# Even attention with turns two and values three items behind the scores, band values in another place, and the last update shared with TensorE

## The reference

```python
def trunk(x, pos, caches, w):
    for l in range(DEPTH):                                   # DEPTH = 2
        g = w['norm_g'][l]
        ff_a = swiglu(rms_norm(x, g[0]), ...)
        x = x + 0.5 * rms_norm(ff_a, g[1])
        h = rms_norm(x, g[2])
        mix, st = even_mixer(h, ...) if l % 2 == 0 else odd_mixer(h, ...)
        x = x + rms_norm(mix, g[3])
        ff_b = swiglu(rms_norm(x, g[4]), ...)
        x = x + 0.5 * rms_norm(ff_b, g[5])
    return x, new_cache_rows
```

```python
s = einsum('bqhd,bkhd->bhqk', q, k) * HEAD_SCALE + bias
p = softmax(where(mask, s, -1e30))
out = einsum('bhqk,bkhd->bqhd', p, v)
```

## Time and profile before

| | |
|---|---|
| time, median of 3 runs | 1887.73 us (1887.36 to 1887.78) |
| the profiled execution, time | 1887.22 us |
| its span, first to last instruction | 1885.4 us |
| TensorE (PE) busy | 1868.0 us, 99% |
| VectorE (DVE) busy | 1529.7 us, 81% |
| ScalarE (ACT) busy | 1183.4 us, 63% |
| GpSimd (POOL) busy | 303.0 us, 16% |

### The profile page before, as it was taken

The page is one execution under the profiler, slowest core; times in us unless marked ns, Lnnn a source line. Parts: engine busy times, 40 slices in busy tenths (PEclk is TensorE's granted clock), DMA queues, the critical chain, the costliest instruction groups (busy, mean ns, idle before and its releaser), DMA issues.

```text
span 1885.4 us, 38908 instructions
## 1 busy us (share of the span) xinstructions
PE 1868.0 (99%) x15552; PEld 1819.0 (96%) x15552; DVE 1529.7 (81%) x2102; ACT 1183.4 (63%) x2281; POOL 303.0 (16%) x317
## 2 busy tenths in 40 slices
PE   9999999999999999999999999999999999999997
PEld 9999999999669999999999999999997999999997
DVE  7889998688773878999868799997757487999975
ACT  7566666765685656666676666666738555656564
POOL 0002020300452100202020002020335200020202
PEclk9999999999999999999999999999999999999999
DMA  4233322422311222322241323233241222232322
GB/s 163 90 107 96 107 96 91 128 69 102 126 46 46 63 95 90 101 102 96 101 129 46 101 97 105 90 112 104 99 126 44 72 65 102 84 118 86 113 93 73
DMA packets 59043, 177.95 MB, mean 94 GB/s; under 512 B 7072, under 2 KB 11504, under 8 KB 58736
## 3 DMA queue, kind: packets, MB, share of 16 engines
q1 hardware_dynamic: 55504, 166.50, 26.3%
q0 software_dynamic: 2128, 7.80, 1.3%
q10 hardware_dynamic: 1232, 1.16, 0.2%
HBM read 168.26 MB, written 5.36 MB: 92 GB/s over the span
## 4 chain that ended last, share of the span: by engine, by line
PE 97%; DMA 1%; DVE 1%; ACT 1%; issue 0%; ACTq 0%; POOL 0%; POOLq 0%; DVEq 0%
PE psum L930 30%; PE psum L928 30%; PE psum L929 30%; PE psum L1295 1%; PE psum L1281 1%; PE psum L1414 1%; PE psum L1199 1%; DMA out_kpe<-kpe_all 1%; PE psum L1397 1%; PE psum L1256 1%; PE psum L1369 1%; PE psum L1245 0%; DMA x<-in_x 0%; PE psum L982 0%; PE psum L1175 0%
## 5 line engine op out<-in xcount | busy, mean ns | idle before, releaser
L928 PE MATMUL psum<-xhi,w_hi 128*128 128x272 f32 x1552 | 451.1, 291 | 1.8 <-DVE xlo L2335 1.7
L930 PE MATMUL psum<-xhi,w_lo 128*128 128x272 f32 x1552 | 447.8, 289 | 0.0
L929 PE MATMUL psum<-xlo,w_hi 128*128 128x272 f32 x1552 | 446.4, 288 | 0.0
L928 PEld LDWEIGHTS psum<-xhi,w_hi 128*128 128x128 f32 x1552 | 292.3, 188 | 5.2 <-issue 2.3
L929 PEld LDWEIGHTS psum<-xlo,w_hi 128*128 128x128 f32 x1552 | 292.2, 188 | 0.5
L930 PEld LDWEIGHTS psum<-xhi,w_lo 128*128 128x128 f32 x1552 | 291.7, 188 | 0.0
L781 DVE TENSOR_TENSOR w_lo<-w_raw,w_hi 128x1024 fp32r<-128x1024 f32 (+1 forms) x208 | 236.7, 1138 | 64.3 <-ACT w_hi L778 61.7
L929 PE MATMUL psum<-corner,w_hi 128*128 128x272 f32 x864 | 249.9, 289 | 0.0
L930 PE MATMUL psum<-corner,w_lo 128*128 128x272 f32 x864 | 249.8, 289 | 0.0
L928 PE MATMUL psum<-corner,w_hi 128*128 128x272 f32 x864 | 248.7, 288 | 0.0
L778 ACT ACTIVATE w_hi<-w_raw 128x1024 fp32r<-128x1024 f32 (+1 forms) x208 | 206.2, 991 | 39.9 <-PE psum L930 38.5
(11 more groups left out here) (366 smaller groups left out, 4918.9 us busy)
## 6 DMA issues: line engine op xcount, KB each, us to landing
w_raw<-in_w_gate_up SPq DMA_DIRECT2D x172, 512.0 KB, 4.1
w_raw<-in_w_down SPq DMA_DIRECT2D x96, 384.0 KB, 3.7
w_raw<-in_w_down SPq DMA_DIRECT2D x32, 256.0 KB, 2.7
w_raw<-in_even_in SPq DMA_DIRECT2D x16, 512.0 KB, 4.2
w_raw<-in_odd_in SPq DMA_DIRECT2D x10, 512.0 KB, 4.3
w_raw<-in_even_out SPq DMA_DIRECT2D x8, 512.0 KB, 4.3
w_raw<-in_odd_out SPq DMA_DIRECT2D x8, 512.0 KB, 4.2
out_band_kv<-qkvb POOLq DMA_DIRECT2D x1, 2176.0 KB, 9.9
```

What stands on the lines that cost most here:

```text
L928: nc.tensor.matmul(out, s_hi, m_hi, start=first, stop=False, skip_group_check=skip)
L929: nc.tensor.matmul(out, s_hi, m_lo, start=False, stop=False, skip_group_check=skip)
L930: return nc.tensor.matmul(out, s_lo, m_hi, start=False, stop=last, skip_group_check=skip)
```

## The change

Three things are changed together.

1. In even attention, TensorE's round becomes `even_scores(n)`, `turn(n - 2)`, `values(n - 3)`, and begins at n = 2 with the turn of item 0 ahead of the scores of item 3. ScalarE's round becomes `copy_turned(n - 2)`, `exponentials(n)`; the outputs follow one round sooner on ScalarE and VectorE. The rounds are one fewer, so the fourth early part of the output projection stands behind the loop. VectorE's order of maxima and inverses and GpSimd's order stay as they are.
2. `vB` moves to the place of `w_sum` and `rstd`, which are not in use in attention. ScalarE's copies into it no longer wait for the two stores, but for the last scaling of the mixer's tiles (`mix_scaled`).
3. In the last update, four tiles (`TAIL`) of the second half are added by TensorE: it multiplies x by the identity into PSUM, then y * r by the identity on top, tile by tile. ScalarE copies each sum to x and stores the tiles in two pairs from its own queue. VectorE multiplies all eight tiles as before and adds the other four.

```diff
--- before.py
+++ after.py
@@ -256,6 +256,7 @@
 JOBS_IN = (1, 5, 7, 9)
 
 
+TAIL = 4
 A0 = {"even": 0, "odd": N_EVEN}
 O0 = {"even": 0, "odd": len(EVEN)}
 
@@ -315,7 +316,8 @@
         w_raw = place("w_raw", [P, 4, D], F32)
         w_hi = place("w_hi", [P, 4, D], F32R)
         w_lo = place("w_lo", [P, 4, D], F32R)
-        gate_even = place("gate_even", [P, 4, TH], F32, at=cursor[0])
+        w_sum_at = cursor[0]
+        gate_even = place("gate_even", [P, 4, TH], F32, at=w_sum_at)
         w_sum = place("w_sum", [P, 3, D // 2], F32)
         rstd_at = cursor[0]
         rstd = place("rstd", [P, T], F32)
@@ -365,7 +367,7 @@
         probsE = [place("probsE%d" % i, [P, 2, w], F32, at=pr_at + o) for i, (w, o) in
                   enumerate(((384, 7168), (512, 10240), (384, 0)))]
         probsTE = [place("probsTE%d" % i, [P, 2, 512], F32, at=pr_at + o) for i, o in enumerate((3072, 14336))]
-        vB = place("vB", [P, 4, NH * HD], F32, at=arena + 17408)
+        vB = place("vB", [P, 4, NH * HD], F32, at=w_sum_at)
         vB_new = place("vB_new", [P, NH * HD], F32, at=pr_at + 18432)
         bias = [place("bias%d" % p, [P, 2, 2 * P], F32, at=kn_at + 3200 * p) for p in range(4)]
         vB_cache = place("vB_cache", [P, 2, NH * HD], F32, at=qr_at)
@@ -491,6 +493,9 @@
         k_ready = sem("k_ready")
         k_copied = sem("k_copied")
         v_ready = sem("v_ready")
+        tail_scaled = sem("tail_scaled")
+        tail_summed = sem("tail_summed")
+        tail_out = sem("tail_out")
         v_copied = sem("v_copied")
         band_in = sem("band_in")
         vb_turned = sem("vb_turned")
@@ -913,9 +918,9 @@
 
             c = len(SUBS)
             for H in range(2):
-                for k, count in ((0, 2), (2, 2), (4, 2), (6, 2)) if H == 0 else ((0, 2), (2, 2), (4, 2), (6, 1), (7, 1)):
+                for k, count in ((0, 2), (2, 2), (4, 2), (6, 2)) if H == 0 else ((TAIL, 2), (6, 1), (7, 1)):
                     some = slice(k, k + count)
-                    sp.wait_ge(x_ready, 16 * (c - 1) + 8 * H + k + count)
+                    sp.wait_ge(x_ready, 16 * (c - 1) + 8 * H + k - TAIL * H + count)
                     sp.dma_start(outs["y"][:, some, HALF[H]], x[:, some, HALF[H]]).then_inc(y_stored, 16)
             sp.wait_ge(y_stored, 16 * (KD + 1))
 
@@ -1319,18 +1324,19 @@
                                 first = False
                     mm.then_inc(pv_done, 1)
 
-                for n in range(3, N_EVEN + 4):
-                    if n < N_EVEN:
+                for n in range(2, N_EVEN + 3):
+                    if 2 < n < N_EVEN:
                         even_scores(n)
-                    if 3 <= n < N_EVEN + 3:
-                        turn(n - 3)
-                    if n >= 4:
-                        values(n - 4)
+                    if n < N_EVEN + 2:
+                        turn(n - 2)
+                    if n >= 3:
+                        values(n - 3)
                     if n in (N_EVEN, N_EVEN + 2):
 
                         pe.wait_ge(exp_done, N_EVEN if n > N_EVEN else N_EVEN - 1)
                     if n >= N_EVEN:
                         out_early(s, n - N_EVEN)
+                out_early(s, 3)
 
             def swa_scores(s, n):
 
@@ -1609,6 +1615,13 @@
                 out_projection(s)
             post_sum(len(SUBS) - 1, 1)
             post_last(len(SUBS) - 1, 1)
+            pe.wait_ge(y_scaled, 2 * KD * ffn_no(len(SUBS)))
+            for m in range(TAIL):
+                nc.tensor.matmul(psum[:, m, 0:TH], ident[:], x[:, m, HALF[1]], start=True, stop=False)
+            for m in range(TAIL):
+                pe.wait_ge(tail_scaled, m // 2 + 1)
+                nc.tensor.matmul(psum[:, m, 0:TH], ident[:], y[:, m, HALF[1]], start=False,
+                                 stop=True).then_inc(tail_summed, 1)
 
 
         def even_output(k, to):
@@ -1667,9 +1680,9 @@
                 for q in range(2):
                     nc.scalar.activation(relS_hi[:, q, :], hankelS[:, q, :], ACT.Copy).then_inc(rel_high, 1)
 
-            for n in range(N_EVEN + 4):
-                if 3 <= n < N_EVEN + 3:
-                    copy_turned(n - 3)
+            for n in range(N_EVEN + 3):
+                if 2 <= n < N_EVEN + 2:
+                    copy_turned(n - 2)
                 if n < N_EVEN:
                     exponentials(n)
                 if n in REL_STEPS:
@@ -1677,7 +1690,7 @@
                 if n in SPLIT_STEPS["even"]:
                     split_unit(act, "act", G0[2] - 3, SPLIT_STEPS["even"].index(n))
                 for k, (_, _, _, first, count) in enumerate(EVEN):
-                    if n == first + count + 3:
+                    if n == first + count + 2:
                         outputs(k)
 
         def swa_output(k, to):
@@ -2173,7 +2186,7 @@
                     split_group(act, "act", g + 10)
 
                     act.wait_ge(vb_turned, 1)
-                    act.wait_ge(stored, 16 * 2)
+                    act.wait_ge(mix_scaled, MIX_STEPS)
                     for j in range(4):
                         nc.scalar.activation(vB[:, j, :], psum[:, j, :], ACT.Copy).then_inc(vb_copied, 1)
                     act.wait_ge(latents_stored, 16)
@@ -2206,6 +2219,13 @@
                 for m in range(4, KD):
                     mixer_result(s, m, 0)
             boundary(len(SUBS))
+            for m in range(TAIL):
+                act.wait_ge(tail_summed, m + 1)
+                nc.scalar.activation(x[:, m, HALF[1]], psum[:, m, 0:TH], ACT.Copy).then_inc(tail_out, 1)
+                if m % 2:
+                    some = slice(m - 1, m + 1)
+                    act.wait_ge(tail_out, m + 1)
+                    act.dma_start(outs["y"][:, some, HALF[1]], x[:, some, HALF[1]]).then_inc(y_stored, 16)
 
 
         @block.vector
@@ -2245,8 +2265,13 @@
                     two = y[:, 2 * j:2 * j + 2, HALF[H]]
                     return own(nc.vector.tensor_tensor(two, two, r, ALU.mult))
 
-                n = scaled(0)
-                for j in range(KD // 2):
+                tail = TAIL // 2 if c == len(SUBS) and H == 1 else 0
+                for j in range(tail):
+                    dve.wait_ge(y_scaled, 2 * KD * (ffn_no(c) - 1) + KD * H + 2 * j + 2)
+                    two = y[:, 2 * j:2 * j + 2, HALF[H]]
+                    nc.vector.tensor_tensor(two, two, r, ALU.mult).then_inc(tail_scaled, 1)
+                n = scaled(tail)
+                for j in range(tail, KD // 2):
                     n_next = scaled(j + 1) if j + 1 < KD // 2 else None
                     own_wait(n)
                     ones_by_one = c == len(SUBS) and H == 1 and j == KD // 2 - 1
@@ -2688,7 +2713,7 @@
                 maxima(2)
                 value(5)
                 value(6)
-                for n in range(2, N_EVEN + 5):
+                for n in range(2, N_EVEN + 4):
                     if 2 < n < N_EVEN:
                         maxima(n)
                     if n < N_EVEN + 1:
@@ -2701,7 +2726,7 @@
                     if n - 1 in SPLIT_STEPS["even"]:
                         split_unit(dve, "dve", G0[2] - 3, SPLIT_STEPS["even"].index(n - 1))
                     for k, (_, _, _, first, count) in enumerate(EVEN):
-                        if n == first + count + 4:
+                        if n == first + count + 3:
                             outputs(k)
 
             nc.vector.memset(eps[:], EPS).then_inc(gains_ready, 1)
```

## The result

The changed kernel takes 1893.25 us, median of 7 runs (1892.85 to 1894.80), beside 1887.64 for the kernel before in the same series: a ratio of 1.0030, with an interval of 1.0021 to 1.0040. One of the seven runs of the kernel before took 3031.78 us, far off all others, and without it the median would be 1887.58. The profiled execution took 1893.25 us, its span is 1891.4, against 1887.22 and 1885.4. So this execution is 6.0 us longer than the one on which the sum was made. The prediction had 1892.8 as the median, and +5.1 on that execution.

What follows compares the result with a forecast made beforehand. TensorE, busy for 1868.0 of 1885.4 us, was taken as the bound. Attention's new order +8.4, vB -2.0 and the last update -1.3 gave +5.1: 1892.3 on the profiled execution, 1892.8 as the median, range 1888.5 to 1895.8.

Steps and rivals of the forecast that it cites:

- 1.0 to 1.3: Even attention: us by which the scaling of the other band items would be late for a turn two behind.
- 7.0 if item 18 keeps its 2.5 whole: Upper bound in us for waits at items 11 to 19, forecast 6.3, with item 18's scaling 2.5 late.
- The start: Turn of item 0, now ahead of scores 3, waits for VectorE's last copies into vA: +1.0 us.
- 0.4 for signals: Attention loop: GpSimd's signals to a waiting TensorE, over eight waits, cost 0.4 us (0 to 1.1).
- The term of +8.4: New order in even attention: waits at the start and turns sum to 9.7 us, less three old waits of 1.3.
- SyncE's store follows as it did: Kernel's end: VectorE's last addition ends 1.3 us sooner, at 1881.4, and SyncE's store comes after it as before.
- the two branches end together: Last update: VectorE's additions end at 1881.4, ScalarE's second store issue starts by 1881.5; hence -1.3 us taken.
- given back: Rival: VectorE and GpSimd run ahead or later stages make good half the waiting; attention +4.2, total 1888.6; chance 0.12.
- C: Attention: time from TensorE leaving the next item's scores to the end of an item's scaling; 3.83 us for item 14.
- its ring: Rival: late turns delay ScalarE's copies and exponentials until ScalarE leads the attention loop; 1895.3; chance 0.05.
- The savings: Rival: something else holds the copies into vB and the last stores, so neither saving comes; 1896.1; chance 0.06.
- the clock: Rival: repeated idling halves TensorE's clock, band items take up to 2.68 us more each; about 1920; chance 0.03.

Runs made afterwards that it cites:

- the later series: The changed kernel, unchanged, run again beside the kernel before on the same chip as its parts: 1893.31 us, ratio 1.0026.

## Why the prediction was right, and where it was off

**The bound and the mechanism: right.** TensorE sets the pace of the loop, and the scaling of item 14 ends 3.83 us after the next item's scores in both orders (that of item 13 after 3.84 in the new one). Two behind, TensorE has 2.68 us of its own work in that time. The new waits stand where they were put, with GpSimd's scaling as releaser, and every other band item is spared, or nearly. The experiment with the inverse shows the cause: moving that one instruction up, with the order two behind unchanged, took 4.4 of the 8.4 us away. One reading was too even: "1.0 to 1.3" for the other band items leaves out item 13, which would have been 1.49 us late by the trace before (539.91 against 538.42). And its upper bound for items 11 to 19, 7.0 if item 18 keeps its 2.5 whole, is 7.5 by its own terms (6.3 + 1.2).

**The waits, item by item.** The prediction had 0.5 at item 8, 1.4 at 11, 1.2 at 13, 15 and 17, 1.3 at 18, and 0.4, 0.75 and 0.3 at 22 to 24: 8.25 us. The rows show 0.17, 1.15, 1.36, 1.16, 0.84, 1.21, 0.58, 0.49 and 0.59: 7.55. The start shows 1.01 for 1.0. The two short waits add 0.23, and the old ones are gone: 0.42, 0.35 and 0.46, and one of 0.12 at 543.95 that has no bracket, 1.35 in all. That makes 7.55 + 1.01 + 0.23 - 1.35 = 7.4. But from the first scores to the mark the time grew from 1875.07 - 487.58 = 1387.49 to 1881.52 - 485.82 = 1395.70 us, by 8.2. Most of the 0.8 between is the overlap that a waiting TensorE loses: a row of 0.92 us (537.62) is followed after 0.87 where nothing waits, the rows of 0.93 and 1.13 in the trace before after 0.85 and 1.06, so each wait costs 0.05 to 0.08 more than its idle time. Eight more waits than before make 0.4 to 0.6 of that; the rest I can't assign. The overlap stands where the prediction put 0.4 for signals, a term that no row before showed; the signal itself, 0.05, is inside the idle time. The term of +8.4 came out so closely in part by luck: the waits were taken 0.5 too large (8.25 for 7.8 with the short ones), and the overlap, which was left out, made up for much of it.

**vB: the right mechanism, mis-sized.** In the profiled execution it brought 2.1 for the 2.0 predicted, and the new condition held nothing up. Against the median of other series of the kernel before it brought 3.5, because there, by the steps of the times, the wait often cost a spell at 1.2 GHz as well, of 1.6 us in the one that was traced. The step that failed is the reading of one execution's clock: 1.00 behind 2.0 us of idle time was one of two things that can follow such a wait.

**The last update: the term that failed.** Predicted -1.3, measured some -0.4 in the trace and -0.43 alone. VectorE's part came out as worked (1.28 us sooner), TensorE's and ScalarE's branch was in time, and the four loads of `x` cost nothing. The step that failed is "SyncE's store follows as it did": from the last issue to the end it took 2.0 us before (1883.39 to 1885.4) and takes 2.75 now (1888.65 to 1891.4). All the stores come within 2.3 us and hold the DMA engines for 3.25, so the last one stands in a queue. That is read from the windows and the issues; the one experiment that began the stores sooner gained too little to confirm it. That the two branches end together was the sign to look there; I counted when the stores were issued and did not add up what they had to move. The eight tiles are 4 x 272 KB = 1.1 MB, at the measured 366 GB/s 3.0 us.

**Sum.** In the profiled execution: +8.2 - 2.1 - 0.4 and 0.3 us of shift further up, 6.0. The forecast of +5.1 lacks the 0.9 of the last update, and little else. Beside the kernel before of the later series the miss at `vB` (1.5 too little gained) and the one at the last update (0.9 too much) have opposite signs and nearly cancel: +4.6 there, +5.6 in the series of the result. That +5.1 is close to both is in part luck.

**The rivals.** Next to nothing was given back. Item 13's C fell from 4.17 to 3.84, as GpSimd's two DMA issues were now over before its inverse came; but the wait at item 18 was still 1.21 us (1.36 at item 13), and the whole 8.2 stood at the mark, 1300 us later. ScalarE released no wait, so its ring did not close. The savings came, one of them only in part. As for the clock, the windows from 520 to 580 us in the trace after have it at 1.00, so the waits of up to 1.36 us there did no harm in that execution. The Trainium skill, "TensorE: Matmul & The Clock Gate", section "HAM oscillation — how this bites in real kernels", tells of a kernel whose TensorE went back to half its clock in every round, after waits longer than any here. The loop after shows no such fall:

```profile
520.00:580.00 60.00, 52.22 (x570) 33.64 (x570) 38.37 (x71) 46.23 (x127) 32.36 (x27) 1.00 0.11 37
```

At the first scores of the kernel before, the two traces differ: 0.50 came after 1.99 us of idle time in the one, and 1.00 stayed after 2.00 us in the other. The prediction's "doesn't bear it out" was too strong for the wait at the first scores, and it held for the loop. Three of the changed kernel's fifteen runs are some 0.9 us or more above the others (1894.68, 1894.69 and 1894.80), and only these have a mean granted clock of 0.999 in place of 1.000. That would fit such a spell; no trace caught one.

## What to carry to other kernels

For a software pipeline, measure how long after its successor's step an item is ready (here 3.83 us) and set it against the work of the engine that turns it out (2.68): the depth must cover the difference, and where it didn't here, every other item waited for about the whole of it (0.84 to 1.36 us for 1.16). Moving one small instruction up in a helper's program was worth half as much as a stage of depth here (4.4 us of 8.4). At the end of a kernel, add up what the last stores have to move before counting on an engine that finishes sooner.

## What the runs showed of the hardware that I had not expected

After one and the same wait of 2.0 us, TensorE's granted clock stayed at 1.00 in one execution and fell to 0.50 in another, which cost 1.56 us of work behind it. What decides between the two is not shown. And the last 1.1 MB of stores filled all 16 DMA engines, at 366 GB/s in the fullest microsecond, and with VectorE 1.3 us sooner they ended only some 0.4 us sooner.
